# Two weight slots at a time: one instruction splits the high, and one the low halves of two neighbouring slots

## What is computed

```python
def conv_ffn(h, w_up, conv_w, w_down):
    u = dwconv3(h @ w_up, conv_w)            # 2048 -> 2 * 5632
    g, v = jnp.split(u, 2, axis=-1)
    return (jax.nn.silu(g) * v) @ w_down     # 5632 -> 2048
...
    yl = hl @ w_qkv                          # q, k, v for the latent tokens
    kv_c = hc @ w_qkv[:, QK_WIDTH:]          # k, v for the context tokens
...
    mod = jax.nn.silu(cond) @ w_ada + b_ada  # six modulation vectors of each layer
```

## Time and profile before

| | |
|---|---|
| median of 3 runs | 2725.49 us (2724.74 to 2732.68) |
| the profiled execution | 2727.95 us, its span 2726.3 us |
| TensorE busy | 2608.7 us (96%) |
| VectorE busy | 2030.7 us (74%) |
| ScalarE busy | 1290.5 us (47%) |
| GpSimd busy | 244.7 us (9%) |
| read from memory | 619.41 MB, 228 GB/s over the span |
| granted TensorE clock, mean | 0.981 of full speed |

### The profile page before, as it was taken

The page is one execution under the profiler, slowest core; times in us unless marked ns, Lnnn a source line. Parts: engine busy times, 40 slices in busy tenths (PEclk is TensorE's granted clock), DMA queues, the critical chain, the costliest instruction groups (busy, mean ns, idle before and its releaser), DMA issues.

```text
span 2726.3 us, 42805 instructions
## 1 busy us (share of the span) xinstructions
PE 2608.7 (96%) x14306; PEld 2195.2 (81%) x14306; DVE 2030.7 (74%) x2724; ACT 1290.5 (47%) x1730; POOL 244.7 (9%) x349
## 2 busy tenths in 40 slices
PE   6999999998979999999999899999899999999998
PEld 3666788876868888888888788888788888888887
DVE  5676988676778988888666688778888767775543
ACT  4322233477645554545444444445455555554443
POOL 1000222000001111011000011001111000000000
PEclk8999999999989999999999999999999999999998
DMA  8774988433668888888787789778688666665553
GB/s 313 263 248 159 301 272 268 123 93 131 221 195 260 271 265 257 270 265 275 240 252 255 247 250 292 246 246 267 211 270 258 217 187 192 185 192 185 184 182 127
DMA packets 471789, 622.82 MB, mean 228 GB/s; under 512 B 19540, under 2 KB 404982, under 8 KB 470672
## 3 DMA queue, kind: packets, MB, share of 16 engines
q1 hardware_dynamic: 424256, 450.94, 49.9%
q0 software_dynamic: 47120, 170.51, 21.8%
q10 hardware_dynamic: 320, 0.13, 0.0%
HBM read 619.41 MB, written 2.10 MB: 228 GB/s over the span
## 4 chain that ended last, share of the span: by engine, by line
PE 67%; DVE 14%; DMA 8%; issue 6%; ACT 4%; DVEq 1%; SPq 0%; ACTq 0%; POOLq 0%; POOL 0%
PE ps L1673 34%; PE ps L1675 17%; DMA ada_ring<-in_w_ada_dram 7%; PE ps L1663 4%; DVE ada_sum L1052 4%; DVE w_lo L992 4%; PE ps L1664 2%; PE ps L1548 2%; PE ps L1604 2%; PE ps L1605 2%; PE ps L1606 2%; ACT w_hi L513 1%; PE ps L1615 1%; DVE part_a L1219 1%; DMA first_x<-in_w_ada_dram 1%
## 5 line engine op out<-in xcount | busy, mean ns | idle before, releaser
L1673 PE MATMUL ps<-xs,w_hi 128*128 128x512 f32 x3840 | 1363.4, 400 | 48.5 <-DVE w_lo L992 26.4
L513 ACT ACTIVATE w_hi<-raw 128x1024 fp32r<-128x1024 f32 (+1 forms) x800 | 829.1, 1040 | 808.5 <-PE ps L1675 481.7
L992 DVE TENSOR_TENSOR w_lo<-raw,w_hi 128x1024 fp32r<-128x1024 f32 (+1 forms) x800 | 955.2, 1200 | 334.2 <-ACT w_hi L513 332.6
L1675 PE MATMUL ps<-xs,w_lo 128*128 128x256 f32 x3840 | 1074.0, 280 | 0.0
L1673 PEld LDWEIGHTS ps<-xs,w_hi 128*128 128x128 f32 x3840 | 724.1, 189 | 231.6 <-DVE w_lo L992 33.3
L1675 PEld LDWEIGHTS ps<-xs,w_lo 128*128 128x128 f32 x3840 | 726.8, 189 | 3.3 <-issue 3.1
L1673 PE MATMUL ps<-act,w_hi 128*128 128x512 f32 x1408 | 495.8, 397 | 0.0
L1675 PE MATMUL ps<-act,w_lo 128*128 128x256 f32 x1408 | 394.7, 280 | 0.0
L1052 DVE SCALAR_TENSOR_TENSOR ada_sum<-ada_ring,cond,ada_sum 128x512 f32<-128x512 f32 x455 | 341.2, 750 | 44.4 <-DMA ada_ring<-in_w_ada_dram 34.5
L431 POOL DMA_DIRECT2D ada_ring<-in_w_ada_dram x264 | 191.1, 724 | 1398.5 <-DVE ada_sum L1052 1345.6
L1673 PEld LDWEIGHTS ps<-act,w_hi 128*128 128x128 f32 x1408 | 264.2, 188 | 63.0
(11 more groups left out here) (200 smaller groups left out, 2428.3 us busy)
## 6 DMA issues: line engine op xcount, KB each, us to landing
raw<-in_ffn_w_up_dram SPq DMA_DIRECT2D x352, 512.0 KB, 4.7
ada_ring<-in_w_ada_dram POOLq DMA_DIRECT2D x264, 512.0 KB, 4.8
raw<-in_ffn_w_down_dram SPq DMA_DIRECT2D x128, 512.0 KB, 4.0
raw<-in_attn_w_qkv_dram SPq DMA_DIRECT2D x96, 512.0 KB, 5.1
raw<-in_sconv_w_in_dram SPq DMA_DIRECT2D x96, 512.0 KB, 5.3
raw<-in_ffn_w_down_dram SPq DMA_DIRECT2D x64, 384.0 KB, 3.3
ada_ring_kv<-in_w_ada_dram POOLq DMA_DIRECT2D x40, 512.0 KB, 6.0
raw<-in_attn_w_o_dram SPq DMA_DIRECT2D x32, 512.0 KB, 4.7
```

Of the source, the lines that this page charges most:

```text
L513: nc.scalar.activation(w_hi[:, slot, 0:n_tiles, :], raw[:, slot, 0:n_tiles, :], ACT.Copy).then_inc(hi_made, 1)
L992: nc.vector.tensor_tensor(w_lo[:, slot, 0:n_tiles, :], raw[:, slot, 0:n_tiles, :], w_hi[:, slot, 0:n_tiles, :], ALU.subtract).then_inc(lo_ ...
L1673: mm(ps[:, bank + m, :], w_hi[:, slot, t, cols], src[:, tile + t, :], start=(is_first and t == 0), stop=False)
L1675: last = mm(ps[:, bank + m, 0:T], w_lo[:, slot, t, cols], src[:, tile + t, 0:T], start=False, stop=(is_last and t == n_tiles - 1))
```

## The change

From K on, `hi` and `lo` do nothing at even slots. At an odd slot they make both slots of the pair (`slot - 1`, `slot`) with one instruction of 2048 elements a partition (2 x 768 for the units of 3 tiles). The pair's `hi` waits for both loads, and for the same count of `w_used` that the odd slot alone waited for; `lo` waits for the same count of `hi_made`. The counters go up by 2. V keeps single instructions (`hi_v`, `lo_v`, which are the old functions). Loads, matmuls and the order of all else are the same; TensorE's, GpSimd's and SyncE's instructions don't change.

```diff
             def hi(quad, slot, n_tiles=KU):
 
+                if slot % 2 == 0:
+                    return
+                pair = slice(slot - 1, slot + 1)
+                se.wait_ge(raw_full[slot - 1], 16 * quad + 16)
+                se.wait_ge(raw_full[slot], 16 * quad + 16)
+
+                wait(se, w_used, 4 * quad + slot - 3)
+                nc.scalar.activation(w_hi[:, pair, 0:n_tiles, :], raw[:, pair, 0:n_tiles, :], ACT.Copy).then_inc(hi_made, 2)
+
+            def hi_v(quad, slot, n_tiles=KU):
+
                 se.wait_ge(raw_full[slot], 16 * quad + 16)
 
                 wait(se, w_used, 4 * quad + slot - 3)
...
             def lo(quad, slot, n_tiles=KU):
 
+                if slot % 2 == 0:
+                    return
+                pair = slice(slot - 1, slot + 1)
+                ve.wait_ge(hi_made, 4 * quad + (slot + 1))
+                nc.vector.tensor_tensor(w_lo[:, pair, 0:n_tiles, :], raw[:, pair, 0:n_tiles, :],
+                                        w_hi[:, pair, 0:n_tiles, :], ALU.subtract).then_inc(lo_made, 2)
+
+            def lo_v(quad, slot, n_tiles=KU):
+
                 ve.wait_ge(hi_made, 4 * quad + (slot + 1))
```

More of the change, by code:

```diff
@@ L517, in _ @@
             copy_rows(0)
-            hi(0, 0)
+            hi_v(0, 0)
             modulate(0, 0)
-            hi(0, 1)
+            hi_v(0, 1)
             modulate(0, 1)
@@ L535, in _ @@
                     if n + 2 < V_UNITS:
-                        hi((n + 2) // 4, (n + 2) % 4)
+                        hi_v((n + 2) // 4, (n + 2) % 4)
                     if 2 <= n < 10:
@@ L1013, in _ @@
             add_mods(0)
-            lo(0, 0)
+            lo_v(0, 0)
             low_h(0, 0)
-            lo(0, 1)
+            lo_v(0, 1)
             low_h(0, 1)
@@ L1063, in _ @@
                     if n + 2 < V_UNITS:
-                        lo((n + 2) // 4, (n + 2) % 4)
+                        lo_v((n + 2) // 4, (n + 2) % 4)
                     if n >= 10:
```

## The result

The changed kernel takes 2890.59 us (median of 4 runs, 2884.85 to 2892.42) where the kernel before, run beside it, takes 2729.09 us: a ratio of 1.0587, 95% interval 1.0563 to 1.061, thus 161 us slower. The profiled execution took 2892.31 us, its span is 2890.3. The forecast was 2820 us with a range up to 2885: right in direction and in the chain that costs, 70 us too small; the terms that fell short, above all `up` with chunks and Q, are named behind the experiments.

What follows compares the result with a forecast made beforehand. TensorE was taken to set the time, with the splitting hidden. Losses of 7.7 + 42 + 4.9 + 26 + 10 + 2 + 4 = 96.6 us on the profiled 2727.95 gave 2824.6, as median about 2820 us; range 2750 to 2885.

Steps and rivals of the forecast that it cites:

- `up` with chunks: Loaded fours of `up0` and `up1`: VectorE's order makes TensorE stop; 2.8 us a four, 15 fours, 42 us lost.
- Q: Attention's Q phase: low half (2, 3) lengthens the head's chain, 16 us, plus 10 us of slow clock; 26 us lost.
- Price of a pair: ScalarE 1.91 us, VectorE 2.27 us a pair; frees 0.08 us of VectorE each, 384 pairs, about 32 us.
- `up` without chunks: Seven fours of `up1`: high pair behind the `SiLU` stops TensorE 0.55 us once in two slabs; 7.7 us lost.
- clock term: In Q, half clock behind TensorE's longer gaps ahead of units 2 and 0: 1.6 us a slab, 10 us.
- `dn0`, `dn1`: Two units of 3 tiles pass in 4.16 us, less than the pair's 4.46: 14 stops of 0.35 us, 4.9 us lost.
- `sin`, `so`, the rest: Late loads and delayed pairs in `sin` 10 us, chunks in `so` 2, norm tails and first K pair 4.
- Two made units instead of three: A pair needs both slots free, so only two made units lie ahead of TensorE; delays over 1.1 us stop it.
- The bounds: Limits around the forecast's terms: `up` 35 to 62 us, Q 16 to 36, `sin` 2 to 13; total 2775 to 2865.
- Larger instructions pay: Rival: VectorE's freed 32 us help the loaded halves, a lead of two suffices; about 2705 us, 5 in 100.
- hidden: Rival: points stand in idle time of both engines, gains and losses cancel; 2718 to 2734 us, 4 in 100.
- late loads: Rival: a pair waits for the later of its two loads, up to 120 us more; 2870 to 2940 us, 13 in 100.

Runs made afterwards that it cites:

- e13: Changed kernel with the `SiLU` issued behind the pair instead of ahead of it: 2861.65 us, 1.0484 of the kernel before.
- e5: Changed kernel with chunk loads of 16 instead of 512 columns from the attention output on: 2844.44 us, 1.0432 of the kernel before.
- e6: Kernel before the change with chunk loads of 16 instead of 512 columns: 2695.15 us, 0.9894 of the kernel before.
- e9: Changed kernel with single halves at the pair's place, the first high half also waiting for the second slot: 2800.8 us, 1.0282 of the kernel before.
- e1: Changed kernel with two single high and two single low halves at the odd slot instead of pairs: 2798.97 us, 1.0295 of the kernel before.
- e14: Changed kernel with high pairs, single low halves at the odd slot and the `SiLU` behind the pair: 2814.83 us, 1.0323 of the kernel before.
- e16: Kernel before the change with three extra matmuls ahead of unit 0 of each Q slab but the first: 2724.58 us, 0.9996 of the kernel before.
- e2: Changed kernel with single high halves at their old places, only low halves in pairs: 2837.93 us, 1.0433 of the kernel before.
- e3: Changed kernel with the pair made at the even unit's turn, ahead of both units' points: 2917.24 us, 1.0716 of the kernel before.
- e10: Changed kernel with high halves in pairs but low halves as two single instructions at the odd slot: 2839.9 us, 1.0437 of the kernel before.

## Why the forecast was right or wrong

- **Price of a pair: right** (1.91 and 2.29 us for 1.91 and 2.27; VectorE freed of 30 us for 32), and so was the verdict that this gain buys nothing.
- **`up` without chunks: mechanism right, size low.** Seven fours lost 1.9 us each, 13.3 us for 7.7. The stop is 0.52 us in two slabs for 0.55 (start to start, 0.42 us ahead of the first matmul and 0.10 us in it); the other 0.42 are a slower pace of TensorE's matmuls, which the forecast did not know of and which may not come from the change (last section). e13 removes the stop alone, 46.3 to 45.2 us a four.
- **`up` with chunks: the term failed by its size, 61 us for 42.** `up0` lost 46 and the loaded fours of `up1` 15 us. The step was the choice of 2.8 us a four, near the low end, "since a slower four gives the loads more time". It does not: e5 and e6 show the loads' delay whole in both orders, and the upper end 4.1 was right. The count itself (45.4 and 49.5) met what e6 and e5 measured (45.7 and 50.1), though it had low (4, 5) follow the chunk at once: the trace has 1.1 us of waiting for the high pair behind the `SiLU`, and e13 gives back 1.5 us a four.
- **Q: failed, 47 us for 26.** The step that failed is the clock term of 1.6 us a slab, and with it "the other half keeps its 12.5 us", which is true at full clock alone. In most slabs both units behind the gaps run at half clock, 1.5 us each, so a later slab loses 3.4 + 3.0 us. The term was read from one gap; the same trace has such a gap without half clock, and the gaps came out shorter than forecast (2.26 and 2.70 us for 4 and 3), so the clock's price could not have been told from it. And the first two slabs, at 18.7 and 19.4 us before, lose over 9 each, where I had taken all like the later ones. The chain itself was near (3.4 us for 2.7).
- **`dn0`, `dn1`: failed in `dn0`, 13 us for 2.4**; `dn1` has 3 for 2.4. The forecast gave both the same stop. `dn0`'s stops are 0.6 to 1.9 us a slab, and weight loads are late in front of them.
- **`sin`, `so`, the rest: 17, 4 and 6 us for 10, 2 and 4.** In `sin` 10 to 14 of the 17 are there with single halves at the pair's place (e9, e1), thus mostly place and not length; with small chunk loads the change costs 9.
- **"Two made units instead of three": no cause of its own that shows.** e9 has that lead and costs no more than e1 within the noise. What costs is that with it a pair's chain of 4.46 us and whatever stands ahead of it must fit into 5.54.
- **The bounds** failed with the terms: `up` measured 74 us for 35 to 62, Q 47 for 16 to 36. Of the 67 us that the sum lacks, `up` with chunks has 19 and Q 21.
- **Rivals.** "Larger instructions pay" and "hidden" fell; "late loads" may hold for some of `dn0`, which was not tried; elsewhere `hi` waits for loads about as long as before (38.6 for 29.5 us in `up0`, 41.0 for 44.7 in `sin`). The total fell into that rival's range for other reasons.

## What to carry to other kernels

Before two instructions are made one, sum the chain from the buffer's return to the consumer's start with the doubled durations, and add what stands ahead of them on each in-order queue: here 4.46 of 5.54 us passed alone and failed behind a `SiLU` that waits for another engine. Look where the merged instruction can stand at all: late it starves the consumer, early it blocks what is behind it, and both cost more (80 us for the late place alone) than the start-up saved (30 us of an engine that had slack elsewhere). Where a wait lengthens TensorE's gaps, the half clock can come behind each gap of the chain: bound its price by none and all, and count in the trace how many gaps of that length bring it, not one.

## What the runs showed of the hardware

TensorE has two paces at one granted clock. Windows over two fours (256 pairs of matmuls) at `up1`'s end, of e13, of e14 and then of e16, in all of which TensorE waits for nothing (us, PE busy, granted clock, DMA share, GB/s):

```profile
2370.74:2461.20 90.46, 90.46 (x514) 1.00 0.56 185
```

```profile
2335.30:2424.00 88.70, 88.70 (x514) 1.00 0.62 189
```

```profile
2200.00:2290.46 90.46, 90.46 (x514) 1.00 0.61 185
```

The same 514 matmuls at clock 1.00 take 90.46 or 88.70 us, 0.353 or 0.347 us for a pair of matmuls. The pace holds through the whole end of `up1`: the kernel before, e1, e9 and e14 have the fast one, the changed kernel, e2, e3, e10 and e13 the slow one. With low pairs in `up1` it was always slow, but e10 is slow with single low halves, e14, which differs from it in the `SiLU` alone, is fast, and e16 is slow with no pair anywhere. e16's profiled execution was the slowest of 12 (2740.54 us, median 2724.58), and its other executions have no trace, so the pace may be one execution's and not the kernel's. The cause stays open; nothing here was made to set it. It is worth 0.9 us a four, some 6 us in the seven fours without chunks, and these are not shown to be part of the change's 161.
